# The low half of the weights' split, computed on VectorE at placed points of every stage

## What is computed

```python
h = layer_norm(x, ln_in_g, ln_in_b)
u = h @ w_in[l]
u_glu, z, xbc, dt_raw, gate_a, gate_b = split_in(u)
y_a = conformer_branch(u_glu, ...)     # a*sigmoid(g), 31-tap causal conv, layer norm, silu, @ w_conv_out
y_b = ssd_branch(z, xbc, dt_raw, ...)  # 4-tap conv, silu, chunked state-space scan, gated group norm, @ w_ssm_out
mix = (sigmoid(gate_a) * y_a + sigmoid(gate_b) * y_b) @ w_o[l]
h = layer_norm(DN_ALPHA * h + mix, ...)
h = layer_norm(DN_ALPHA * h + conv_ffn(h, ...), ...)   # @ w_up, 3-tap conv, silu(gate)*val, @ w_down
...
for l in range(DEPTH_2):                # second block, two layers
    proj = rmsnorm(h) @ w_in[l]         # q, k, v, b_gate, c_gate, hc
    y = concat(rmsnorm(sliding_window_attention(q, k, v)), rmsnorm(b_gate * conv(c_gate * hc)))
    h = h + rmsnorm(y @ w_out[l])
    h = h + rmsnorm(square(relu(rmsnorm(h) @ w_up[l])) @ w_down[l])
```

## Time and profile before

| | |
|---|---|
| median of 3 runs | 2549.59 us (2546.25 to 2555.57) |
| the profiled execution, its span | 2546.4 us |
| TensorE busy | 2278.3 us, 89% |
| VectorE busy | 1397.0 us, 55% |
| ScalarE busy | 1016.5 us, 40% |
| GpSimd busy | 949.7 us, 37% |
| mean granted TensorE clock | 0.948 of full |

### The profile page before, as it was taken

One profiled execution on the slowest core, in us unless ns is written; L12 is line 12 of the kernel. 1 busy time (PEld: TensorE's weight loads), 2 busy tenths in 40 slices (PEclk: granted clock), 3 DMA queues, 4 the chain that ended last, 5 costly groups with the idle time before them and its releaser, 6 DMA issues.

```text
span 2546.4 us, 34303 instructions
## 1 busy us (share of the span) xinstructions
PE 2278.3 (89%) x12362; PEld 1939.2 (76%) x12362; DVE 1397.0 (55%) x1514; ACT 1016.5 (40%) x1391; POOL 949.7 (37%) x253
## 2 busy tenths in 40 slices
PE   5998898878779799999789889999988988999996
PEld 3786676756658588878589879999988876778875
DVE  5637888899966433431355556306426565740633
ACT  4455555553252455542435533313223353331331
POOL 2333234336524144455432134343434223434431
PEclk9999999989889799999899889999999989999998
DMA  3232222211112122224221112222222111122221
GB/s 121 88 109 79 91 77 92 74 66 66 67 65 94 38 99 99 99 101 145 85 86 49 36 67 84 83 88 94 83 95 75 50 50 67 67 99 99 83 99 49
DMA packets 34492, 207.44 MB, mean 81 GB/s; under 512 B 4802, under 2 KB 4802, under 8 KB 10980
## 3 DMA queue, kind: packets, MB, share of 16 engines
q1 hardware_dynamic: 28128, 194.66, 21.7%
q10 hardware_dynamic: 6276, 11.57, 1.4%
HBM read 204.05 MB, written 2.17 MB: 81 GB/s over the span
## 4 chain that ended last, share of the span: by engine, by line
PE 64%; DVE 18%; DVEq 8%; ACT 4%; issue 3%; POOL 2%; ACTq 1%; DMA 0%; POOLq 0%
PE PS L505 20%; PE PS L507 19%; PE PS L509 19%; DVE vout L1578 5%; DVEq L1571 4%; POOL wlo L430 1%; PE PS L820 1%; DVEq L1474 1%; DVE hres L1475 1%; PE PS L846 1%; ACT whi L914 1%; DVE zres L1473 1%; DVE rstd L1465 1%; DVE rl L1966 1%; DVEq L1594 1%
## 5 line engine op out<-in xcount | busy, mean ns | idle before, releaser
L430 POOL TENSOR_TENSOR wlo<-raw,whi 128x2048 fp32r<-128x2048 f32 x181 | 842.2, 4653 | 1416.7 <-ACT whi L914 1398.9
L505 PE MATMUL PS<-ahi,whi 128*128 128x512 f32 (+1 forms) x2472 | 764.9, 350 | 89.4 <-DVE alo L1459 39.0
L507 PE MATMUL PS<-alo,whi 128*128 128x512 f32 (+1 forms) x2472 | 750.5, 344 | 0.0
L509 PE MATMUL PS<-ahi,wlo 128*128 128x512 f32 (+1 forms) x2472 | 748.2, 343 | 0.0
L914 ACT ACTIVATE whi<-raw 128x2048 fp32r<-128x2048 f32 x179 | 342.8, 1915 | 660.7 <-PE PS L509 655.3
L505 PEld LDWEIGHTS PS<-ahi,whi 128*128 128x128 f32 x2472 | 434.8, 193 | 165.8 <-issue 87.7
L507 PEld LDWEIGHTS PS<-alo,whi 128*128 128x128 f32 x2472 | 434.4, 192 | 52.5 <-issue 2.0
L509 PEld LDWEIGHTS PS<-ahi,wlo 128*128 128x128 f32 x2472 | 433.4, 192 | 52.6
L1578 DVE SCALAR_TENSOR_TENSOR vout<-vpad,cols,vout (+1 forms) x216 | 272.0, 1281 | 32.2 <-issue 31.6
L1966 DVE TENSOR_TENSOR rl<-rl,rstd 128x528 f32<-128x528 f32 (+1 forms) x64 | 149.0, 2328 | 248.3 <-ACT rl L1353 247.5
L505 PE MATMUL PS<-f2hi,whi 128*128 128x264 f32 (+1 forms) x768 | 205.9, 322 | 2.0 <-DVE f2lo L1972 1.8
(11 more groups left out here) (250 smaller groups left out, 2811.2 us busy)
## 6 DMA issues: line engine op xcount, KB each, us to landing
raw<-weights SPq DMA_DIRECT2D x181, 1024.0 KB, 4.8
acs_b<-acs_rows ACTq DMA_DIRECT2D x34, 256.0 KB, 3.2
const<-const ACTq DMA_DIRECT2D x2, 1232.0 KB, 6.0
x_in<-x_t SPq DMA_DIRECT2D x4, 512.0 KB, 5.2
out_t<-hres SPq DMA_DIRECT2D x8, 256.0 KB, 2.0
cols<-columns SPq DMA_DIRECT2D x1, 385.0 KB, 6.6
const<-const SPq DMA_DIRECT2D x1, 256.0 KB, 6.7
acs_rows<-dtt ACTq DMA_DIRECT2D x1, 64.0 KB
```

What stands on the lines that cost most here:

```text
L430: nc.gpsimd.tensor_tensor(wlo[s][:, :], raw[s][:, :], whi[s][:, :].bitcast(F32), ALU.subtract).then_inc(lo_ready, 1)
L505: nc.tensor.matmul(o, wh, h, start=first, stop=False)
L507: nc.tensor.matmul(o, wh, h, start=False, stop=False)
L509: mm = nc.tensor.matmul(out[j], wl, hi[j], start=False, stop=last)
```

## The change

GpSimd's `lows` and `z_low` go. GpSimd keeps `gated`, the adds of the long convolution's last tile and the sums of squares, and its `low` for single units: the second unit of ffn_up and of each layer's in and up0, five in all by the code, each of which now waits for `lo_ready` of the unit before it as well. VectorE gets the same subtraction as `low`, with `low_at` for a fixed unit and `low_next` for the unit after next of a loop. Its calls stand at fixed points: ahead of the evacuation in xbc, ffn_up and the up stages, between heads and taps in z_glu, between the two halves of the sums of y squared, in the norm of y, in the middle and at the end of a turn of ssm_out's loop (whose taps are now four and three), in `layer_norm` ahead of the reciprocal and between its low parts, behind the evacuation in conv_out, w_o and down1, and around it in ffn_down; in a layer ahead of `row_scale`, behind the scaling of v, behind `gated(0)`, at the end of every second step of the attention, and between the sums of squares in out. In down0, where VectorE had nothing to do, it has a loop of its own. Some loops are opened up so that the units kept by GpSimd can be left out. No data, buffer, DMA or semaphore is added. SP's loads wait for the same counts of `lo_ready` as before.

```diff
@@ -425,29 +425,13 @@
...
         def _(pool):
-            def low(s, value):
-                hold(pool, hi_ready, value, "pool")
-                nc.gpsimd.tensor_tensor(wlo[s][:, :], raw[s][:, :], whi[s][:, :].bitcast(F32),
+            def low(u):
+                pool.wait_ge(hi_ready, u + 1)
+                pool.wait_ge(lo_ready, u)
+                nc.gpsimd.tensor_tensor(wlo[u % 2][:, :], raw[u % 2][:, :], whi[u % 2][:, :].bitcast(F32),
...
-            def lows(first, end):
...
-                if first % 2:
-                    low(1, first + 1)
-                if (first + 1) // 2 < end // 2:
-                    with pool.Fori((first + 1) // 2, end // 2) as i:
-                        for s in range(2):
-                            low(s, 2 * i + s + 1)
-                if end % 2:
-                    low(0, end)
...
-            stage = PLAN["z_glu"]
-            n = stage.n // GROUPS
-            lows(0, stage.u0 + 2)
             with pool.Fori(0, GROUPS) as g:
-                def z_low(u):
-                    low(stage.slot(u % 2), g * n + (stage.u0 + u + 1))
@@ -455,21 +439,12 @@
...
-                z_low(2)
-                z_low(3)
-                gated(0)
-                gated(1)
-                z_low(4)
-                gated(2)
-                gated(3)
-                z_low(5)
...
-            first = PLAN["ssm_out"].u0
-            lows(stage.u0 + stage.n + 2, first + 1)
+                for j in range(GP):
+                    gated(j)
...
                 for s in range(2):
-                    low((first + s + 1) % 2, 2 * i + (first + s + 2))
@@ -486,13 +461,11 @@
...
-            done = first + POOL_TURNS + 1
+            low(PLAN["ffn_up"].u0 + 1)
...
                 for stage, n, span in ((f"in_{l}", y["n_pre"], every), (f"up0_{l}", y["n_mpre"], span_of(l))):
-                    lows(done, PLAN[stage].u0 + 2)
+                    low(PLAN[stage].u0 + 1)
                     add_squares(n, span)
-                    done = PLAN[stage].u0 + 2
-            lows(done, UNITS)
@@ -1397,11 +1370,26 @@
...
+            def low(s, n, after_pool=None):
...
+                hold(dve, hi_ready, n + 1, "dve")
+                if after_pool is not None:
+                    dve.wait_ge(lo_ready, after_pool)
+                v.tensor_tensor(wlo[s][:, :], raw[s][:, :], whi[s][:, :].bitcast(F32), ALU.subtract
+                                ).then_inc(lo_ready, 1)
...
+            def low_at(u, after_pool=False):
+                low(u % 2, u, u if after_pool else None)
...
+            def low_next(stage, i, s):
...
+                low(stage.slot(s), 2 * i + (stage.u0 + s + 2))
...
-            def layer_norm(n, src, hi, lo, each=None, pe_odd=True):
+            def layer_norm(n, src, hi, lo, each=None, pe_odd=True, units=(), late=None):
@@ -1414,11 +1402,15 @@
...
                         v.tensor_tensor(acc1[:, :], acc1[:, :], sq1[(k - 1) % 2][:, :], ALU.add).then_inc(n["dve"].sem, 1)
+                for u in units:
+                    low_at(u)
...
-                def low(k):
+                def act_low(k):
+                    if late and k == late[0]:
+                        low_at(late[1])
@@ -1429,10 +1421,10 @@
...
                     if hi is not None and k >= 2:
-                        low(k - 2)
+                        act_low(k - 2)
                 if hi is not None:
-                    low(KD - 2)
-                    low(KD - 1)
+                    act_low(KD - 2)
+                    act_low(KD - 1)
@@ -1488,13 +1480,15 @@
...
                 add_up(x_in[:, k * T:(k + 1) * T], xin_ok)
-            layer_norm(n_in, x_in, ahi, alo)
+            layer_norm(n_in, x_in, ahi, alo, units=(0, 1))
+            low_at(2)
...
                 slot = stage.slot(s)
+                low_next(stage, i, s)
@@ -1614,6 +1608,7 @@
...
                                 causal.unsqueeze(1).to_broadcast([P, CHUNKS, P]), ALU.mult).then_inc(cbm_ok, 1)
+                low_next(stage, 2 * g, 0)
@@ -1631,6 +1626,10 @@
...
                     s = q % 2
+                    if q == 4:
+                        low_next(stage, 2 * g, 1)
+                    if q == 6:
+                        low_next(stage, 2 * g + 1, 0)
@@ -1639,26 +1638,32 @@
...
                 long_taps([2 * g], TAPS_AT[-1], TAPS)
+                low_next(stage, 2 * g + 1, 1)
...
-            with dve.Fori(0, GROUPS) as g:
-                acc = cut(sumsq, T * g, T)
-                for j in range(GP):
-                    hold(dve, ysq_ok, GP * g + (j + 1), "dve")
-                    if j == 0:
-                        v.tensor_copy(acc, ysq[0][:, :]).then_inc(ysq_sum, 1)
-                    else:
-                        drain()
-                        v.tensor_tensor(acc, acc, ysq[j % 2][:, :], ALU.add).then_inc(ysq_sum, 1)
+            stage_b = PLAN["gate_b"]
+            for half in range(2):
+                with dve.Fori(half * GROUPS // 2, (half + 1) * GROUPS // 2) as g:
+                    acc = cut(sumsq, T * g, T)
+                    for j in range(GP):
+                        hold(dve, ysq_ok, GP * g + (j + 1), "dve")
+                        if j == 0:
+                            v.tensor_copy(acc, ysq[0][:, :]).then_inc(ysq_sum, 1)
+                        else:
+                            drain()
+                            v.tensor_tensor(acc, acc, ysq[j % 2][:, :], ALU.add).then_inc(ysq_sum, 1)
+                low_at(stage_b.u0 + half + 2)
...
             def y_low(k):
+                if k in (0, GP):
+                    low_at(stage_b.u0 + 4 + k // GP)
@@ -1683,19 +1688,24 @@
...
             assert 4 * n + TAPS_GATE == TAPS
+            stage_s = PLAN["ssm_out"]
             with dve.Fori(0, KD // 2) as i:
-                long_taps(odd, 0, n, n * i + TAPS_GATE)
                 for s in range(2):
+                    long_taps(odd, (n + 1) // 2 * s, n if s else (n + 1) // 2, n * i + TAPS_GATE)
+                    low_next(stage_s, i, s)
...
                     v.tensor_tensor(t, t, ring[s][:, :], ALU.mult).then_inc(ring_used, 1)
+            stage_a = PLAN["gate_a"]
...
                 add_up(vout[:, u * T:(u + 1) * T], vout_ok)
+            low_at(stage_a.u0 + 2)
...
             add_up(vout[:, POOL_TILE * T:(POOL_TILE + 1) * T], vout_ok)
-            layer_norm(n_conv, vout, chi, clo, pe_odd=False)
+            low_at(stage_a.u0 + 3)
+            layer_norm(n_conv, vout, chi, clo, pe_odd=False, units=(stage_a.u0 + 4,), late=(4, stage_a.u0 + 5))
@@ -1714,6 +1724,7 @@
...
                     v.tensor_tensor(cut(gb, c, T), cut(gb, c, T), cut(ga, c, T), ALU.add).then_inc(mix_ok, 1)
+                low_next(stage_c, i, s)
@@ -1741,9 +1752,12 @@
...
                     add_up(cut(res1, c, T), r1_ok)
+                if 2 * i + s < stage_w.n - 1:
+                    low_next(stage_w, i, s)
...
             v.memset(acc1[:, :], 0.0)
-            unit_loop(dve, stage_w, w_o_unit)
+            for u in range(stage_w.n):
+                w_o_unit(u // 2, u % 2)
@@ -1751,6 +1765,10 @@
...
                 slot = stage_u.slot(s)
+                if isinstance(i, int) and i == 0 and s == 0:
+                    low_at(stage_u.u0 + 2, True)
+                else:
+                    low_next(stage_u, i, s)
@@ -1766,19 +1784,31 @@
...
-            unit_loop(dve, stage_u, up_unit)
+            for u in range(2):
+                up_unit(0, u)
+            unit_loop(dve, stage_u, up_unit, 2)
...
             v.memset(acc1[:, :], 0.0)
-            with dve.Fori(0, KD // 2) as i:
...
+            def down_tile(i, t, last=False):
...
+                c = 2 * T * i + t * T
+                low(stage_d.slot(0), 4 * i + (stage_d.u0 + 2 * t + 2))
+                hold(dve, unit_done, 4 * i + (stage_d.u0 + 2 * t + 2), "dve")
+                v.scalar_tensor_tensor(cut(res2, c, T), cut(ahi, c, T).bitcast(F32), ALPHA, bank(4 + 2 * t),
+                                       ALU.mult, ALU.add).then_inc(psum_free[0], 1)
+                drain().then_inc(psum_free[1], 1)
+                v.scalar_tensor_tensor(cut(res2, c, T), cut(alo, c, T).bitcast(F32), ALPHA, cut(res2, c, T),
+                                       ALU.mult, ALU.add)
+                add_up(cut(res2, c, T), r2_ok)
+                if not last:
+                    low(stage_d.slot(1), 4 * i + (stage_d.u0 + 2 * t + 3))
...
+            with dve.Fori(0, KD // 2 - 1) as i:
                 for t in range(2):
-                    c = 2 * T * i + t * T
-                    hold(dve, unit_done, 4 * i + (stage_d.u0 + 2 * t + 2), "dve")
-                    v.scalar_tensor_tensor(cut(res2, c, T), cut(ahi, c, T).bitcast(F32), ALPHA, bank(4 + 2 * t),
-                                           ALU.mult, ALU.add).then_inc(psum_free[0], 1)
-                    drain().then_inc(psum_free[1], 1)
-                    v.scalar_tensor_tensor(cut(res2, c, T), cut(alo, c, T).bitcast(F32), ALPHA, cut(res2, c, T),
```

(27 more changed lines are left out.)

## The result

The changed kernel takes 2469.18 us in the median of four runs (2467.35 to 2470.54), against 2552.3 for the kernel before beside it (2546.25 to 2555.57): a ratio of 0.9682, 95% interval 0.9664 to 0.9700. The profiled execution has a span of 2467.3 us, 79.1 less than that of before. In one later round a single execution of the kernel before took 4527.58 us and one of the kernel with GpSimd's fills 6941.47, where the others of these two kernels took 2545 to 2555 and 2470 to 2472; these two slow executions are left out of what follows.

What follows compares the result with a forecast made beforehand. Most stages were taken as TensorE's, some as VectorE's, stalled by GpSimd's subtractions. Terms -6, +1.5, -18, -5, -23, -6, -3 and -7 sum to -66.5, say -67, from 2549.6: 2482.6 us, own range 2467 to 2498, outer range 2457 to 2512.

Steps and rivals of the forecast that it cites:

- C: Stages VectorE sets: taps stay slow from another cause, 32 subtractions add 74 us, nothing gained, 2624 us; chance 0.03.
- E: Whole kernel: the stalls have another cause and the new work is hidden, no change, 2550 us; chance 0.04.
- C2: Each moved subtraction costs VectorE 4.65 us instead of 2.3, and ffn_up loses its cover: 2596 us; chance 0.01.
- Start: First sums no longer stalled, two subtractions placed in VectorE's idle time before the reciprocal: net -6 us.
- xbc: Subtractions hidden within TensorE's unit, except beside the dt arithmetic and after the last unit: net +1.5 us.
- z_glu: VectorE's cycle shortens by 5.6 us a group, of which 4.5 counted, four times: -18 us, bounds -10 and -30.
- ssm_out: VectorE's loop goes from 126 to 105 us and stays the bound: net -23 us, bounds -12 and -37.
- rival A: z_glu and ssm_out: TensorE takes up all VectorE frees, adds hardly collide, -30 and -37, 2457 us; chance 0.14.
- TensorE's waits for the split later: After ssm_out, TensorE's seven waits for the split, 8.5 us in all, each come 2.3 us sooner: -6 us.
- Attention and up stages: Last units of four up stages, -3 us in all; attention's entry and end in both layers, -7 us.
- Rival B: ssm_out and z_glu: new operations hold up GpSimd's adds and so ScalarE's split, some 28 us, 2510; chance 0.10.
- Rival D: Stalls go, but another wait ends as late, which would halve z_glu and ssm_out: about 2503 us; chance 0.10.

Runs made afterwards that it cites:

- GpSimd's fills: Changed kernel, with GpSimd doing four 512-column constant fills, reading no SBUF, where it subtracted before in z_glu and ssm_out: 2471.75 us.
- the idle subtraction: Changed kernel, plus GpSimd subtractions of constant SBUF tensors that nobody reads, 16 in z_glu and 8 in ssm_out, two operations each: 2565.93 us.
- the doubled subtraction: Changed kernel, with each of VectorE's 176 subtractions done twice into the same place, the unit released after the second: 2671.11 us.
- the quarters: Kernel before, with each GpSimd subtraction cut into four operations of 512 columns and nothing moved to VectorE: 2523.11 us.
- the kernel early: Changed kernel, with ssm_out's subtractions placed earlier in VectorE's loop, behind two of the first four tap batches and one of the last three: 2465.82 us.

## Why the prediction was right

2482.6 was forecast and 2469.2 measured, inside the forecast's own range of 2467 to 2498, near its lower end: the gain in the profiled execution was 79.1 where the sum said 66.5. By its steps:

- **The cause.** GpSimd's subtraction holds up VectorE's two-input operations. Shown by the idle subtraction (nothing needed is later, and 97 us are lost) and by the fills (the same places without reading, 2.6 us lost, where the gating comes later). The prediction had read that the tap ends when the subtraction does; it ends 0.55 us behind it, which changes nothing in the 4.1. Rivals C and E fall with it, and so does the idea that a sooner split is the gain.
- **The price.** 2.30 us estimated, 2.296 measured over 176. C2's 4.65 falls. Its reasoning on cover was sound, though: 7.4 us and a price of 4.65 are more than the 10.9 of a unit, and that is what the doubled subtraction does to ffn_up, 12.5 a unit, 1.5 lost in each.
- **Start**, -6 said, -4.8 measured. The two subtractions fit in front of the reciprocal, which starts at 29.35 instead of 34.60.
- **xbc**, +1.5 said, -1.1 measured to the end of the stage. The wait for the second unit's split went (-1.0). The wait for the last tile, which I had counted at +1.6, is real, but it lies behind the end of xbc: z_glu's first unit takes 20.1 us instead of 18.1, and TensorE stands still 1.5 us longer in it. TensorE's row before and after:

```profile
197.27 0.52 PE L689 MATMUL PS<-const,b_slot 128*128 128x128 f32 x3 [3.80 <-ACT xbc L999]
```
```profile
193.39 0.87 PE L662 MATMUL PS<-const,b_slot 128*128 128x128 f32 x3 [5.27 <-ACT xbc L972]
```

- **z_glu**, -18 said, -23.1 measured, and -25 without that 2.0; this is the largest miss. I had let the rest go to TensorE and counted 4.5 a group; it was 4.1 in the first group, which has the wait above, and 6.1 to 6.7 in the other three. Between the ends of units VectorE's busy time fell by 6.9 a group (63.3 to 56.4) and TensorE's by 1.7 to 2.8, so the group followed VectorE to within 0.8 us: the stalls that went were 16 us and not 15.6, the four subtractions cost 9.1 and not 10, and TensorE held next to nothing back. The granted clock rose from 0.95 to 0.98 in these groups to 1.00. So rival A was half right, and I had put that into a rival instead of into the term. In the other kernels, with the same products, the clock is the lower the more VectorE holds the group up: 1.00 at 67.7 us with the fills, 0.98 at 71.6 with the quarters, 0.93 to 0.94 at 77.5 to 79.4 with the doubled subtraction, where GpSimd subtracts nothing, and 0.92 at 80.5 to 81.8 with the idle one. That the clock rose because the waits went is borne out by these; what it gave in time isn't shown, since VectorE's 6.9 cover the gain alone.
- **gate_b and the norm of y**, -5 said, -6.7 measured.
- **ssm_out**, -23 said, -23.0 measured, with the loop at 104.8 against the 105 that I had worked out. Two errors cancel in it: I had priced 19 adds at 0.76, 14.4, and they cost 18.2; and the eight subtractions at 2.5, 20, where they take 2.28 each, 18.2, when nothing holds them, and start without the gap of 0.2 that I had added. That VectorE stays the bound was right; placing the work elsewhere in the loop moved TensorE's wait and not the time. That wait was not foreseen: I had named 4 us of waits for the split as a sign, and there are 16.8, of which 11.8 stand in front of unit 35. That they cost next to nothing is what the kernel early shows.
- **TensorE's waits for the split later**, -6 said. The waits are gone as said: 8.5 us from 885 on the earlier trace rows, and in the changed kernel no such wait is listed for TensorE from 830 on, the same place. Not all of it is gain: at unit 55 the wait for the split turned into one for the taps of the 3-tap convolution, which on VectorE now stand behind the subtraction, and this unit ends no sooner. I had named the wait that goes, and not the one that is late next.

```profile
834.48 0.47 PE L478 MATMUL PS<-ahi,whi 128*128 128x512 f32 x1 [3.47 <-DVE fg L1390]
```

- **Attention and up stages**, with the line above -16 said, -20.5 measured behind 885 us: the two stages in with the attention 6.9, out 7.0, up and down 5.9, ffn_down 1.1, less 0.5 at the end. Of the attention's part, 2.7 lie in the attention of the second layer, between the ends of units 136 and 141, and that stretch takes 76.1 to 80.7 us in kernels that do the same work in it; it can't be claimed for the change. kpad is at 0.71 us instead of 4.84, but TensorE's idle time before it is 5.1 instead of 5.85: 0.7 came back and not the 1.9 that I had counted, because VectorE, in front of the subtraction, also waits 1.17 us for ScalarE's whi:

```profile
1260.34 2.29 DVE L1378 TENSOR_TENSOR wlo<-raw,whi 128x2048 fp32r<-128x2048 f32 x1 [1.17 <-ACT whi L887]
```

  The sums of squares at the other end gave more than their share: one of 528 columns has a mean of 708 ns, where it had 1505. No kernel here gives the subtractions of in and out back to GpSimd, so that these 14 us are the collisions' is argued from such rows.
- **Nothing in ffn_up, conv_out and w_o**: 0.0 measured. Right. The 94 subtractions of ffn_up, ffn_down and the up and down stages, given back to GpSimd, cost 6.1 us at most.
- **Rival B**, the blocking turned round, is real and small: GpSimd's add at 627.57 in the idle kernel. In the changed kernel GpSimd's adds have a mean of 1465 and 1564 ns, before 1509 and 1518; they reach the 1.5 at which B should begin, and nobody waits longer for them: ScalarE's whi in ssm_out follows TensorE's units.
- **Rival D**, another wait as late: at unit 55, and in part at the attention's entry. In z_glu the split is there when VectorE comes for it: no subtraction of the group above has idle time before it.

The sum was 66.5 and the gain 79.1. The 12.6 between them are z_glu with 5.1, the part behind 885 us with 4.5, xbc with 2.6 and the norm of y with 1.7, less 1.2 at the start. All but the last err in the same direction, so the total doesn't owe its place in the range to errors that cancel; the exact hit of ssm_out does.

## What to carry to other kernels

When an engine's group has a mean far over the free length of the same shape, look for what runs beside it before counting its work: here 176 subtractions could be given to an engine that looked half busy, because 336 us of its busy time were being held up by them. Count such a move stage by stage, with what VectorE costs where it is waited for, and measure the slack where it is hidden: 2.3 us a unit were free in ffn_up, and the next 2.3 cost 1.5 each. An idle copy of the suspected operation, with a result that nobody reads, separates contention from readiness in a single run.
